# Modulation columns made later: eight column units moved into attention, four into the second feed-forward, and the third group's products reordered

## The chip, the cores and the metric

The kernel runs on one core of one Trainium2 chip. The metric is device time in microseconds (us) of one execution. TensorE is PE in the rows, VectorE DVE, ScalarE ACT, GpSimd POOL; SyncE is SP, which here issues the weight transfers.

## What is computed

A transformer of 256 tokens and width 1024 in fp32. Two layers of a first block come first, each with four mixers side by side (a latent attention, a stick-breaking attention, a block-sparse attention and a gated convolution) and an output product. Then comes a second block: a gated linear attention (GLA), feed-forward 0, an attention of 16 heads in chunks, feed-forward 1. The four stages of the second block are modulated: a vector `c` goes through SiLU and a matrix `w_ada_2`, and gives each stage `s` (0 GLA, 1 feed-forward 0, 2 attention, 3 feed-forward 1) a shift, a scale and a gate. In the reference, cut to that:

```python
...
h = ln(x) * (1 + scale) + shift
x = ln(ALPHA * x + gate * stage(h))
...
```

The shift and scale of a stage are wanted at its input, the gate at its end.

## The kernel before, in words

**The stream of weights.** All weights come as 180 units of 128 x 2048 floats (1 MB) in one fixed order, into a ring `raw` of six slots (`SLOTS = 6`). Unit n goes to slot n % 6. SP issues the units strictly in their order, in one loop at L483: unit n is issued once whoever reads unit n-6 has counted up `used[n % 6]`. So a unit that is read late holds up the issue of the unit six places on, and of all behind that. The strings `ORDER`, `GLA_ORDER`, `FF_ORDER` (and the new `ATT_ORDER`) say what stands where: `w`, `m`, `u` and `d` are weights for TensorE, `a` is a column unit.

**The column units.** `w_ada_2` is 48 of the units. `column_unit` (L982) multiplies a unit with the row `crow` = SiLU(c) on VectorE and sums along the row, in two instructions of 128 x 1024; the second one counts the slot free. No other engine reads these units. Per stage there are eight units for shift and scale (`acc`) and four for the gate (`gacc`); `coefficients(s)` makes the vectors of stage s from its eight, a short operation `gcol` those of its gate from its four. Before, 24 are made in the two layers of the first block (12 each), 11 in GLA, 13 in feed-forward 0, none later.

**Each engine runs its own program** in the written order and waits on semaphores. So where `ada_unit` stands in VectorE's program, everything behind it on VectorE waits for the unit to land and for its two instructions.

**Layer boundary.** At the end of layer 0, `y_norm` gives the new rows, TensorE transposes a tile of 128 tokens (`first_transposes`), ScalarE scales the eight transposed blocks into `hT` (`layer_input`), and TensorE multiplies (`first_units`), tile by tile; `unit_t` of unit `U_CA` comes behind both tiles. `y_square` is a ScalarE operation of the normalisation of the layer that ends.

**GLA's end.** VectorE's program has three column units (8, 9, 10 of GLA), then `mixer_output`, which reads the output product from PSUM; its row results `xs` are what TensorE transposes for feed-forward 0 (L2057).

**Feed-forward.** 16 groups; the products run as seven products of four quarter blocks. Per group TensorE runs of the next group's up products a "first tile", a "half" and a "rest", and of this group's down products part 0 (two products, from the hidden half sums alone) and part 1 (five: one that needs the hidden sums, four that need `weight_sums`, made by VectorE). The "half" waits for the sums of the up weights that VectorE makes in `up_sums` (L1590 to L1595).

**Attention.** Four passes `qd` of four heads. A pass (`four_heads`) runs the scores, softmax, turns (transposes of the probabilities, L1998) and values of four heads, and between them three units `quad_unit(u)` (L2625) that make queries, keys and values of the next pass. GpSimd's program in a pass is `quad_weights(3 qd + 3)` (four sums over the weights of a unit, L578 to L583, once that unit has landed), `head_biases(qd + 1)` (L593 to L596, which ends in a count of `cur_ready`), then `quad_weights` of the next two units. VectorE's program in a pass is: `scores_max`, `head_inverse` of heads 0 and 1, `quad_sums`, `scores_max`, `queries`, `head_inverse` (L1056) of heads 2 and 3, `quad_sums` (L1864 to L1873), `x_piece` or the output weights, `quad_sums`, the copy L1943, `value_rows(qd + 1)` (L1894), which waits for `cur_ready`; then the scores of the next pass (L1046).

Of the kernel before, what the change touches and what calls it, by code (L numbers as in the profile page):

```python
# [14 lines left out]
P = 128  # L15
# [22 lines left out]
A1 = 12  # L38
# [5 lines left out]
ORDER = "wwwawwawwawawawa" "wawawawa" "wwawwa"  # L44
# [37 lines left out]
GLA_ORDER = 4 * "mma" + "mmaaaa" + "mmmmmmaaa"  # L82
FF_ORDER = ("u" + 13 * "uda" + "ud" + "dud", "u" + 14 * "ud" + "dud")
# [3 lines left out]
N_FF1 = N_ATT + 16  # L87
# [10 lines left out]
AG = len(GA_AT)  # L98

ADA_1 = [N_GLA + n for n in GA_AT] + places(FF_ORDER[0], "a", N_FF0)  # L100
assert len(GW_AT) == 16 and len(ADA_1) == 24
# [34 lines left out]
def build(nc, x, units, cols, small, post_g, consts, onehot, rel_bias, crow_in, colb_in,  # L136
          ln_rows, low_in, gk_in, att_line, v_row, out):
    with ExitStack() as ctx:  # L138
# [13 lines left out]
        HB = ((G[2], G[3]), (G[0], G[1]))  # L152
# [114 lines left out]
        early = sb("early", [P, 4, P])  # L267
# [167 lines left out]
        OUT_UNITS.append(tuple(N_ATT + 12 + w for w in range(4)))  # L435
# [7 lines left out]
        OUT_W.append([[ada[:], xs[:, 1, :], row(tline), crow[:]],  # L443
# [46 lines left out]
        def _(pool):  # L490
# [57 lines left out]
            store_gate(0)  # L548
            for l in range(1, DEPTH):
                layer_vectors(l)  # L550
            store_gate(1)

            pool.wait_ge(x_new.sem, 2 * DEPTH + 2)
            for g in range(2):
                load_gate(g)
# [7 lines left out]

            norm_rows(1)
# [4 lines left out]
            def quad_weights(u):  # L569

                n = N_ATT + 3 + u
# [4 lines left out]
                if u >= 3:  # L576
                    wait_used(pool, 0, n - 3)
# [27 lines left out]

            store_gate(3)
            load_gate(3)
# [17 lines left out]
            norm_rows(2)  # L625
            norm_rows(3)

        @block.scalar
        def _(act):
# [79 lines left out]
            for l in range(DEPTH):  # L709
# [201 lines left out]
            def keys(qd):  # L911
                act.wait_ge(bc_ready.sem, bc_ready.at(qd, 1))
                if qd == 0:
                    wait_used(act, 0, N_ATT + 1)
# [42 lines left out]
        def _(dve):  # L957
# [31 lines left out]
            def gate_columns(g, n):  # L989

                wait_used(dve, 0, n)
                dve.wait_ge(colb_ready, 16)
                dve.scalar_tensor_tensor(gcol[:, g, :], gacc[:, g, :], 1.0, colb[:, B_GATE + KC * g:B_GATE + KC * (g + 1)],
                                         ALU.add, ALU.add).then_inc(gcol_ready, 1)

            def ada_unit(l, a):

                n = l * U1 + A_AT[a]
                if a < 4:
                    column_unit(n, gacc[:, l, 2 * a:2 * a + 2])  # L1000
                    if a == 3:
                        gate_columns(l, n)
                else:
                    column_unit(n, acc[:, 0, 16 * l + 2 * (a - 4):16 * l + 2 * (a - 4) + 2])
# [54 lines left out]
            def coefficients(s):  # L1059
# [3 lines left out]
                wait_used(dve, 0, (A_AT[A1 - 1], U1 + A_AT[A1 - 1], ADA_1[19], ADA_1[19])[s])  # L1063
# [104 lines left out]
            for l in range(DEPTH):  # L1168
# [12 lines left out]
                if l > 0:  # L1181
                    ada_unit(l - 1, 11)
                    ada_unit(l, 0)
# [16 lines left out]
                if l == 0:  # L1200
                    silu_row()
                    ada_unit(l, 0)
                ada_unit(l, 1)
# [6 lines left out]
                ada_unit(l, 2)  # L1210
                dve.wait_ge(xg_ready.sem, xg_ready.at(l, 1))
                taps(0, 12)
                ada_unit(l, 3)
# [12 lines left out]
                ada_unit(l, 4)  # L1226
# [12 lines left out]
                ada_unit(l, 5)  # L1239
                ada_unit(l, 6)  # L1240
# [37 lines left out]
                for j in range(2 * H):  # L1278
                    if j % 2 == 0:
# [15 lines left out]
                        if j < 6:  # L1295
                            ada_unit(l, 7 + j // 2)
# [36 lines left out]
                ada_unit(l, 10)  # L1333
# [20 lines left out]
                else:  # L1354
                    ada_unit(l, 11)

            def ada_unit_1(n, idx):

                part, i = idx // 4, idx % 4
                if part in (2, 5):  # L1360
                    g = DEPTH + part // 3
                    column_unit(n, gacc[:, g, 2 * i:2 * i + 2])
                    if i == 3:
                        gate_columns(g, n)
                else:
                    m = (0, 1, 3, 4).index(part)
                    column_unit(n, acc[:, 1, m * KC + 2 * i:m * KC + 2 * i + 2])
# [310 lines left out]

            def groups(s):
# [6 lines left out]
                for g in range(SEVEN - 1):  # L1686
# [8 lines left out]
                    weight_sums(down[g])  # L1695
# [57 lines left out]
            ada_unit_1(ADA_1[0], 0)  # L1753
# [3 lines left out]
            coefficients(1)  # L1757
            ada_unit_1(ADA_1[1], 1)
# [3 lines left out]
            ada_unit_1(ADA_1[2], 2)  # L1762
# [22 lines left out]
            ada_unit_1(ADA_1[3], 3)  # L1785
# [4 lines left out]
            ada_unit_1(ADA_1[4], 4)  # L1790
            mixer_sums(6)
            ada_unit_1(ADA_1[5], 5)
# [22 lines left out]
            for a in (6, 7):  # L1815
                ada_unit_1(ADA_1[a], a)
# [29 lines left out]
            for a in (8, 9, 10):  # L1846
                ada_unit_1(ADA_1[a], a)
# [12 lines left out]
            def quad_sums(u, c):  # L1860

                b = [x[:].rearrange("p (i n) -> p i n", i=4) for x in QUAD_BANKS[u % 3]]
                wait_used(dve, 0, N_ATT + 3 + u)
# [13 lines left out]
            def queries(qd):  # L1877
                dve.wait_ge(bc_ready.sem, bc_ready.at(qd, 1))
                if qd == 0:
                    wait_used(dve, 0, N_ATT)  # L1880
# [1017 lines left out]
```

## Time and profile before

| | |
|---|---|
| median of three runs | 976.6 us (975.53 to 977.18) |
| the profiled execution | 975.87 us, span of its records 974.0 us |
| TensorE busy | 957.1 us, 98% of the span |
| VectorE busy | 758.5 us, 78% |
| ScalarE, GpSimd busy | 230.7 us, 83.7 us |
| moved by DMA | 205.38 MB |

The span runs from the first to the last recorded instruction of the profiled execution; the 1.9 us by which that execution is longer lie around it. Busy time of an engine is the time in which one of its instructions runs. "Idle" in brackets behind a row of a timeline is how long the engine stood still ahead of it, and the name behind the arrow what released it.

### The profile page before, as it was taken

The numbers are of one execution on the slowest core, as the hardware profiler recorded it, in microseconds if no ns is written. First come the engines' busy times: TensorE is split into PE (matmuls) and PEld (weight loads), VectorE is DVE, ScalarE is ACT, GpSimd is POOL, SyncE is SP. The second block draws the span as 40 slices with busy tenths as digits, with TensorE's granted clock in tenths as the row PEclk, the third lists the DMA queues.
The fourth block names the chain that finished last, engine by engine and source line by source line (L and its number), as shares of the span: only waits on it lengthen the run. The fifth ranks groups of instructions, "written<-read, shape, count | busy, mean of one in ns | idle before, by whom it ended". The sixth has DMA issues, their size and how long they took to land. (4 is left out here: it accounts for less than half of the span.)

```text
span 974.0 us, 14339 instructions
## 1 busy us (share of the span) xinstructions
PE 957.1 (98%) x5354; PEld 711.0 (73%) x5354; DVE 758.5 (78%) x1719; ACT 230.7 (24%) x580; POOL 83.7 (9%) x100
## 2 busy tenths in 40 slices
PE   9999999999999999999999999999999999999996
PEld 5858855858857998757777777689994767777764
DVE  2796687696688898999999888955667877766687
ACT  4134425125433222111000000123333200000002
POOL 2100000000001000000001000056830000000000
PEclk9999999999999999999999999999999999999999
DMA  9954653855555766574779777535444254544411
GB/s 354 379 201 191 234 201 149 350 197 226 196 215 209 288 220 257 178 297 149 245 289 336 284 257 259 189 131 195 152 173 147 103 184 173 216 173 174 173 44 44
DMA packets 31069, 205.38 MB, mean 211 GB/s; under 512 B 3640, under 2 KB 4845, under 8 KB 7709
## 3 DMA queue, kind: packets, MB, share of 16 engines
q1 hardware_dynamic: 27740, 190.94, 52.9%
q0 software_dynamic: 3264, 13.57, 3.9%
q8 instruction: 43, 0.70, 0.3%
q14 instruction: 22, 0.17, 0.1%
HBM read 203.42 MB, written 1.07 MB: 210 GB/s over the span
## 5 line engine op out<-in xcount | busy, mean ns | idle before, releaser
L1971 PE MATMUL bank<-hT,raw 128*128 128x256 f32 x736 | 162.5, 380 | 0.0
L1971 PEld LDWEIGHTS bank<-hT,raw 128*128 128x128 f32 x736 | 138.9, 190 | 21.2 <-issue 2.4
L982 DVE CUSTOM_DVE_ANT_0 raw<-raw,crow 128x1024 f32<-128x1024 f32 x96 | 113.2, 1222 | 6.7 <-DMA raw<-units_dram 5.3
L2315 PE MATMUL bank<-yT,arena 128*128 128x512 f32 x224 | 100.8, 593 | 0.1
L2315 PE MATMUL bank<-raw,arena 128*128 128x512 f32 x180 | 86.8, 593 | 0.0
L2315 PEld LDWEIGHTS bank<-yT,arena 128*128 128x128 f32 x224 | 42.5, 190 | 54.0 <-issue 51.9
L2342 PEld LDWEIGHTS bank<-hT,raw 128*128 128x128 f32 x416 | 50.4, 192 | 11.5 <-issue 11.5
L839 ACT ACTIVATE arena<-bank 128x512 f32<-128x512 f32 x26 | 15.6, 598 | 179.3 <-PE bank L2342 179.3
L2342 PE MATMUL bank<-hT,raw 128*128 128x128 f32 x416 | 50.6, 275 | 0.0
L1024 DVE SCALAR_TENSOR_TENSOR arena<-arena 128x256 f32<-128x256 f32 x120 | 49.2, 485 | 0.1
L2342 PE MATMUL bank<-arena 128*128 128x128 f32 x336 | 42.2, 275 | 3.0 <-issue 3.0
L2342 PEld LDWEIGHTS bank<-arena 128*128 128x128 f32 x336 | 39.8, 192 | 4.6 <-issue 4.6
L2342 PE MATMUL bank<-arena,gateT 128*128 128x128 f32 x336 | 42.1, 275 | 0.0
L2315 PEld LDWEIGHTS bank<-raw,arena 128*128 128x128 f32 x180 | 29.9, 191 | 16.3 <-issue 16.3
L2342 PEld LDWEIGHTS bank<-arena,gateT 128*128 128x128 f32 x336 | 39.8, 192 | 0.0
L2040 PE MATMUL bank<-arena 128*128 128x512 f32 x88 | 39.7, 592 | 0.0
L2342 PEld LDWEIGHTS bank<-arena,raw 128*128 128x128 f32 x224 | 29.4, 192 | 13.4 <-issue 13.4
L841 ACT ACTIVATE arena<-bank 128x384 f32<-128x384 f32 x28 | 13.8, 492 | 106.8 <-PE bank L2342 106.8
L2286 PE MATMUL bank<-hT,raw 128*128 128x128 f32 x244 | 37.4, 283 | 1.3 <-ACT hT L700 1.1
L2286 PEld LDWEIGHTS bank<-hT,raw 128*128 128x128 f32 x244 | 33.0, 191 | 4.3 <-issue 3.0
L1602 DVE TENSOR_TENSOR arena<-arena 128x256 f32<-128x256 f32 x26 | 11.4, 440 | 31.0 <-ACT arena L839 30.8
L2040 PEld LDWEIGHTS bank<-arena 128*128 128x128 f32 x88 | 16.6, 190 | 19.8 <-issue 19.7
(471 smaller groups left out, 1767.9 us busy)
## 6 DMA issues: line engine op xcount, KB each, us to landing
raw<-units_dram SPq DMA_DIRECT2D x178, 1024.0 KB, 4.9
arena<-ln_rows_dram POOLq DMA_DIRECT2D x4, 1024.0 KB, 5.0
arena<-gate_scratch POOLq DMA_DIRECT2D x4, 512.0 KB, 5.5
arena<-att_line_dram POOLq DMA_DIRECT2D x4, 512.0 KB, 5.8
arena<-small_dram POOLq DMA_DIRECT2D x2, 896.0 KB, 10.5
raw<-units_dram SPq DMA_DIRECT2D x2, 704.0 KB, 7.5
xt<-x_dram SPq DMA_DIRECT2D x2, 512.0 KB, 5.4
arena<-post_g_dram POOLq DMA_DIRECT2D x2, 512.0 KB, 8.4
```

The source lines that it names most:

```text
L839: act.activation(prod[:, 0:4].rearrange("p i n -> p (i n)"), A[0][:], ACT.Copy).then_inc(prod_ready.sem, 1)
L841: act.activation(prod[:, 4:7].rearrange("p i n -> p (i n)"), A[0][:, 0:3 * P], ACT.Copy).then_inc(prod_ready.sem, 1)
L982: ins = dve.tensor_tensor_reduce(out=w, in0=w, in1=crow[:], scale=1.0, scalar=0.0, op0=ALU.mult, op1=ALU.add, accum_out=dst[:, c:c + 1])
L1024: ins = dve.scalar_tensor_tensor(cacc[:, c, :], xg[:, c, j:j + S], w, cacc[:, c, :], ALU.mult, ALU.add)
L1602: ch.do(dve.tensor_tensor(csum[:, 0:5:4], p[:, 0:1].to_broadcast([P, 2, P]), p[:, 1:3], ALU.add))
L1971: mm = pe.matmul(b[:, c * S:(c + 1) * S], raw[:, s, k * 256 + c * P:k * 256 + (c + 1) * P], act_t[:, k, :], start=(k == 0), stop=(k == KC ...
L2040: mm = pe.matmul(OUT_BANKS[l][j][:], x[c] if isinstance(x, list) else x[:, c], y[c] if isinstance(y, list) else y[:, 512 * c:512 * (c + 1) ...
L2286: mm = pe.matmul(b[:, c * S + t * P:c * S + (t + 1) * P], raw[:, n % SLOTS, k * 256 + c * P:k * 256 + (c + 1) * P], hT[:, k, t * P:(t + 1) ...
L2315: mm = pe.matmul(SB[i][:], x, y, start=g == 0, stop=stop)
L2342: mm = pe.matmul(b[:, i * P:(i + 1) * P], x(k), y(k), start=k == 0, stop=k == 3)
```

## The change

Column units are numbered through all four stages now (`ADA_AT`, `ada_unit(i)`): the two layers of the first block make six each (GLA's twelve), GLA makes twelve (feed-forward 0's), feed-forward 0 twelve (attention's), attention eight (shift and scale of feed-forward 1), feed-forward 1 four (its own gate). In attention they stand behind `head_inverse` of head 3: two in pass 0, three in pass 1, three in pass 2. `coefficients` 1, 2 and 3 move with them. At the layer boundary `layer_input` is issued in two halves around the second `y_square`, and `U_CA`'s product is made per tile (`first_columns`), its first half ahead of the second tile's transposes. At GLA's start the second tile's transposes are issued two products earlier. In the feed-forwards' group 1 the two products of part 0 are issued ahead of the "half", and the product with the hidden sums ahead of the "rest"; VectorE makes `weight_sums` of that group a group earlier. Two small loads of the gate rows (`store_gate`, `load_gate`) move later on GpSimd.

```diff
-A1 = 12
+A2 = 12
+A1 = 6
...
-ORDER = "wwwawwawwawawawa" "wawawawa" "wwawwa"
+ORDER = "wwwawwa" "wwwawwa" "wwawwa" "wwww"
...
-GLA_ORDER = 4 * "mma" + "mmaaaa" + "mmmmmmaaa"
-FF_ORDER = ("u" + 13 * "uda" + "ud" + "dud", "u" + 14 * "ud" + "dud")
+GLA_ORDER = 4 * "mma" + "mmaaaa" + "mmmmmmaaaa"
+ATT_ORDER = "www" "aa" "wwwa" "aa" "wwwa" "aa" "wwwwwww"
+FF_ORDER = ("u" + 2 * "ud" + "aua" + 10 * "dua" + "du" + "ddud",
+            "u" + 2 * "ud" + "aua" + 2 * "dua" + 9 * "du" + "ddud")
...
+ATT_UNITS = ((0, 1), (2, 3, 4), (5, 6, 7), ())
...
-        HB = ((G[2], G[3]), (G[0], G[1]))
+        HB = ((G[2], G[3]), (A[2], A[3]))
...
                     y_square(l, 1, 0)
+                    layer_input(l + 1, 0, 0, KC // 2)
                     y_square(l, 1, 1)
-                    layer_input(l + 1, 0, 0, KC)
+                    layer_input(l + 1, 0, KC // 2, KC)
...
+            def ada_unit(i):
+
+                n, g, j = ADA_AT[i], i // A2, i % A2
+                if j < 2 * H:
+                    column_unit(n, acc[:, g // 2, 16 * (g % 2) + 2 * j:16 * (g % 2) + 2 * j + 2])
                 else:
-                    column_unit(n, acc[:, 0, 16 * l + 2 * (a - 4):16 * l + 2 * (a - 4) + 2])
+                    column_unit(n, gacc[:, g, 2 * (j - 2 * H):2 * (j - 2 * H) + 2])
+                if j == A2 - 1:
+                    wait_used(dve, 0, n)
+                    dve.wait_ge(colb_ready, 16)
+                    dve.scalar_tensor_tensor(gcol[:, g, :], gacc[:, g, :], 1.0, colb[:, B_GATE + KC * g:B_GATE + KC * (g + 1)],
+                                             ALU.add, ALU.add).then_inc(gcol_ready, 1)
...
+            def side_unit(lay, g):
+
+                if g < (AH - AF0, len(ADA_AT) - AF1)[lay]:
+                    ada_unit((AF0, AF1)[lay] + g)
+                    if lay == 0 and g == 2 * H - 1:
+                        coefficients(2)
...
                     up_half_sums(s, g + 1)
-                    weight_sums(down[g])
+                    if g == 1:
+                        side_unit(lay, 0)
+                    else:
+                        weight_sums(down[g])
                     up_rest_sums(s, g + 1)
                     hidden_sums(s, g + 1, (g + 1) % 3)
                     if g < SEVEN - 2:
                         up_sums(up[g + 2], g + 2)
                     else:
                         weight_sums(down[SEVEN - 1], wsum_last)
+                    if g == 0:
+                        wait_used(dve, 0, down[0])
+                        weight_sums(down[1])
                     if 1 <= g <= 4:
                         x_piece(s - 1, g - 1)
...
-                    if lay == 0 and AG + g < len(ADA_1):
-                        ada_unit_1(ADA_1[AG + g], AG + g)
-                        if AG + g == len(ADA_1) - 1:
-                            coefficients(2)
-                            coefficients(3)
+                    if g > 0:
+                        side_unit(lay, g)
...
-            coefficients(1)
-            ada_unit_1(ADA_1[1], 1)
...
             for a in (6, 7):
-                ada_unit_1(ADA_1[a], a)
+                ada_unit(GA + a)
+            coefficients(1)
...
-            for a in (8, 9, 10):
-                ada_unit_1(ADA_1[a], a)
+            for a in (8, 9, 10, 11):
+                ada_unit(GA + a)
 
             mixer_output(MIXER, MIX_S, OUT_BANKS[MIXER])
...
                 head_inverse(h0, 3)
+                for a in ATT_UNITS[qd]:
+                    ada_unit(AH + a)
+                    if a == 2 * H - 1:
+                        coefficients(3)
                 if qd == H - 2:
                     dve.wait_ge(oq_ready.sem, 2)
                     out_inputs(HEADS, 0)
...
+            def first_columns(turns, n, b, t):
+
+                wait_landed(pe, turns, n)
+                for c in range(2):
+                    for k in range(KC):
+                        mm = pe.matmul(b[:, c * S + t * P:c * S + (t + 1) * P],
+                                       raw[:, n % SLOTS, k * 256 + c * P:k * 256 + (c + 1) * P],
+                                       hT[:, k, t * P:(t + 1) * P], start=(k == 0), stop=(k == KC - 1))
+                if t == NT - 1:
+                    mm.then_inc(used[n % SLOTS], 1)
...
                     first_units(l, t)
+                    if l > 0 and t == 0:
+                        first_columns(T1 * l, U_CA, G[0], t)
...
-                unit_t(T1 * l, U_CA, hT, G[0])
+                if l > 0:
+                    first_columns(T1 * l, U_CA, G[0], 1)
+                else:
+                    unit_t(T1 * l, U_CA, hT, G[0])
...
-                if part != 0:
+                if part != 0 and stage != "weights":
                     pe.wait_ge(hsum_ready.sem, hsum_ready.at(s // 2, g + 1))
                     product(2, hsum[:, k, 3], b[1][1])
+                if part != 0 and stage != "input":
...
                     if g > 1:
                         up_products(s, n, g + 1, "first tile")
+                    if g == 1:
+                        seven_products(s, down[g], g, 0)
                     if g > 0:
                         up_products(s, n, g + 1, "half")
-                    seven_products(s, down[g], g, 0)
+                    if g == 1:
+                        seven_products(s, down[g], g, 1, stage="input")
+                    else:
+                        seven_products(s, down[g], g, 0)
                     up_products(s, n, g + 1, "rest")
-                    seven_products(s, down[g], g, 1)
+                    seven_products(s, down[g], g, 1, stage="weights" if g == 1 else None)
...
                 for k in range(KC):
+                    if t == 0 and k == KC - 2:
+                        input_transposes(1)
                     mm = unit_columns(n, G[1], t, 1)(k)
                 if t == NT - 1:
                     mm.then_inc(used[n % SLOTS], 1)
-                if t == 0:
-                    input_transposes(1)
```

The engines' programs show where instructions went. First VectorE in pass 0 of attention, before: `head_inverse` of heads 2 and 3 (L1056), then at once `quad_sums` (L1864 on).

```order
L1056 RECIPROCAL rinv<-rsum 128x2 x2
L1864 COPY arena<-bank 128x128
L1866 TENSOR_TENSOR arena<-arena,bank 128x2x128
L1868 TENSOR_TENSOR arena<-arena,bank 128x128
L1869 TENSOR_TENSOR arena<-arena,bank 128x128
```

The same place of VectorE's program after the change; L991 is `column_unit`, with two rows for each of its instructions (the second reads out the sum), L1530 is `x_piece`.

```order
L1061 RECIPROCAL rinv<-rsum 128x2 x2
L991 ISA raw,acc<-raw,crow 128x1024
L991 ISA acc 128x1
L991 ISA raw,acc<-raw,crow 128x1024
L991 ISA acc 128x1
L991 ISA raw,acc<-raw,crow 128x1024
L991 ISA acc 128x1
L991 ISA raw,acc<-raw,crow 128x1024
L991 ISA acc 128x1
L1860 COPY arena<-bank 128x128
L1862 TENSOR_TENSOR arena<-arena,bank 128x2x128
```

Two whole column units now stand between the two. In passes 1 and 2 there are three at that place.

Next TensorE at the boundary from layer 0 to layer 1, before: L2012 are the transposes of a tile, L2024 its first units, L1971 are `unit_t` of U_CA, U_CG and U_BQ.

```order
L2012 MATMUL bank<-kst,xs 128x128 x8
L2024 MATMUL bank<-raw,hT 128x352 x8
L2012 MATMUL bank<-kst,xs 128x128 x8
L2024 MATMUL bank<-raw,hT 128x352 x8
L1971 MATMUL bank<-hT,raw 128x256 x48
```

After, with `first_columns` as L2036:

```order
L2012 MATMUL bank<-kst,xs 128x128 x8
L2024 MATMUL bank<-raw,hT 128x352 x8
L2036 MATMUL bank<-hT,raw 128x128 x16
L2012 MATMUL bank<-kst,xs 128x128 x8
L2024 MATMUL bank<-raw,hT 128x352 x8
L2036 MATMUL bank<-hT,raw 128x128 x16
L1971 MATMUL bank<-hT,raw 128x256 x32
```

Sixteen of the 48 products have moved, in two halves by tile, one of them between the tiles.

## Rows read from the trace of the kernel before

**Rows 1.** The page's first part: busy us, share of the span, instructions.

```profile
PE 957.1 (98%) x5354; PEld 711.0 (73%) x5354; DVE 758.5 (78%) x1719; ACT 230.7 (24%) x580; POOL 83.7 (9%) x100
```

**Rows 2.** TensorE's waits: us in total, times, longest.

```profile
PE bank L2024 <- ACT hT L685: 1.5, 2, 1.3
PE bank L2286 <- ACT hT L700: 1.1, 3, 0.4
PE bank L2057 <- DVE xs L1419: 0.2, 1, 0.2
```

**Rows 3.** VectorE: first unit at GLA's end, what follows; first operation of `coefficients(3)`.

```profile
413.97 1.22 DVE L982 CUSTOM_DVE_ANT_0 raw<-raw,crow 128x1024 f32<-128x1024 f32 x1
420.84 0.69 DVE L1153 COPY arena<-bank 128x512 f32<-128x512 f32 x1
607.88 0.18 DVE L1065 TENSOR_TENSOR arena<-acc,colb 128x16 f32<-128x16 f32 x1 [0.21 <-DVE arena L1079]
```

**Rows 4.** Attention, pass 0 into pass 1: start, us, engine, line.

```profile
667.40 1.28 POOL L578 TENSOR_TENSOR arena<-raw 128x512 f32<-128x512 f32 x1 [5.49 <-PE bank L2625]
672.43 0.47 POOL L593 COPY arena<-arena 128x256 f32<-128x256 f32 x1
673.94 0.30 POOL L596 MEMSET arena<- 64x256 f32 x1
676.12 0.29 DVE L1864 COPY arena<-bank 128x128 f32<-128x128 f32 x1 [3.34 <-PE bank L2625]
678.62 2.26 POOL L581 TENSOR_TENSOR gateT<-gateT,raw 128x512 f32<-128x512 f32 x1
685.50 1.83 DVE L1894 TENSOR_TENSOR arena<-arena 128x256 f32<-128x256 f32 x2
686.39 1.95 PE L2625 MATMUL bank<-arena 128*128 128x128 f32 x16
690.86 0.91 PE L1998 MATMUL bank<-kst,probs 128*128 128x128 f32 x6
```

**Rows 5.** The weight queue: one issue; landing times, single and of two issued together.

```profile
417.62 0.33 SPq L483 DMA_DIRECT2D raw<-units_dram  x1
DMA to landing us min/median/max: 4.6/4.6/4.6
DMA to landing us min/median/max: 4.8/5.8/6.8
```

**Rows 6.** Pass 1 into pass 2; window: length, PE, PEld, DVE, ACT, POOL busy.

```profile
696.54:709.36 12.82, 12.82 (x117) 12.05 (x116) 7.60 (x16) 3.25 (x8) 11.39 (x10) 1.00 0.47 150
709.36 1.83 DVE L1894 TENSOR_TENSOR arena<-arena 128x256 f32<-128x256 f32 x2
```

**Rows 7.** Pass 2 into pass 3, from the end of `head_inverse` to the scores.

```profile
719.78:733.89 14.11, 14.11 (x118) 12.54 (x117) 9.82 (x23) 2.96 (x8) 0.85 (x3) 1.00 0.54 194
733.89 0.28 DVE L1046 CUSTOM_DVE_ANT_0 probs<-bank,arena 128x128 f32<-128x128 f32 x1
```

**Rows 8.** TensorE at the layer boundary.

```profile
158.09 1.13 PE L2024 MATMUL bank<-raw,hT 128*128 128x352 f32 x3 [1.32 <-ACT hT L685]
```

**Rows 9.** Feed-forward 0, group 1: TensorE, VectorE and ScalarE around the half.

```profile
456.81 0.69 DVE L1595 TENSOR_TENSOR arena<-raw,arena 128x512 f32<-128x512 f32 x1
457.61 2.02 PE L2342 MATMUL bank<-arena 128*128 128x128 f32 x16 [1.51 <-issue]
464.72 3.60 PE L2315 MATMUL bank<-yT,arena 128*128 128x512 f32 x8
464.06 0.49 ACT L841 ACTIVATE arena<-bank 128x384 f32<-128x384 f32 x1 [4.01 <-PE bank L2342]
469.03 0.69 DVE L1595 TENSOR_TENSOR gateT<-raw,gateT 128x512 f32<-128x512 f32 x1
```

**Rows 10.** Windows at the end of the span; the number before DMA's is the granted clock.

```profile
966.00:970.00 4.00, 0.00 (x0) 0.00 (x0) 3.73 (x12) 1.54 (x3) 0.00 (x0) 0.98 0.32 131
970.00:974.00 4.00, 0.00 (x0) 0.00 (x0) 1.46 (x3) 0.00 (x0) 0.00 (x0) 0.50 0.35 131
```

More of the change, by code:

```diff
@@ L97 @@
 GW_AT, GA_AT = places(GLA_ORDER, "m"), places(GLA_ORDER, "a")
-AG = len(GA_AT)
-ADA_1 = [N_GLA + n for n in GA_AT] + places(FF_ORDER[0], "a", N_FF0)
-assert len(GW_AT) == 16 and len(ADA_1) == 24
+ATT_UNITS = ((0, 1), (2, 3, 4), (5, 6, 7), ())
+ATT_AT = places(ATT_ORDER, "w", N_ATT)
+ADA_AT = [l * U1 + n for l in range(DEPTH) for n in A_AT] + [N_GLA + n for n in GA_AT]
+GA, AF0 = DEPTH * A1, len(ADA_AT)
+ADA_AT += places(FF_ORDER[0], "a", N_FF0)
+AH = len(ADA_AT)
+ADA_AT += places(ATT_ORDER, "a", N_ATT)
+AF1 = len(ADA_AT)
+ADA_AT += places(FF_ORDER[1], "a", N_FF1)
+assert len(GW_AT) == len(ATT_AT) == 16 and (AF0, AH, AF1, len(ADA_AT)) == (24, 36, 44, 48)
 RE = 2 * DEPTH
@@ L434, in build @@
         OUT_UNITS = DEPTH * [(U_O0, U_O1, U_O2, U_O3)] + [tuple(N_GLA + GW_AT[12 + w] for w in range(4))]
-        OUT_UNITS.append(tuple(N_ATT + 12 + w for w in range(4)))
+        OUT_UNITS.append(tuple(ATT_AT[12 + w] for w in range(4)))
         MIXER, HEADS = DEPTH, DEPTH + 1
@@ L547, in _ @@
             pool.tensor_copy(moba_bias[:], zline[:, :, ::-1]).then_inc(fixed_ready, 1)
-            store_gate(0)
             for l in range(1, DEPTH):
                 layer_vectors(l)
-            store_gate(1)
+            store_gate(0)
             pool.wait_ge(x_new.sem, 2 * DEPTH + 2)
-            for g in range(2):
-                load_gate(g)
+            load_gate(0)
             pool.dma_start(ln_row[:].rearrange("p g d -> p (g d)"), ln_rows[0, :, :].to_broadcast([P, 2 * D])).then_inc(lnrow_in, 16)
@@ L625, in _ @@
             norm_rows(2)
+            store_gate(3)
+            load_gate(3)
             norm_rows(3)
@@ L1353, in _ @@
                     x_scale(l + 1, 1)
[L1354 to L1367, printed above, removed]
             def stage_tiles(s, b=None):
@@ L2306, in unit_columns, with seven_products @@
                 return column
-            def seven_products(s, n, g, part=None, stop=False, wsum=wsum):
+            def seven_products(s, n, g, part=None, stop=False, wsum=wsum, stage=None):
                 k = g % 3
@@ L2723, in last_heads @@
                 out_product(HEADS, 1, 3)
[L2725 to L2726 removed]
+            wait_landed(pe, 0, ATT_AT[2])
+            unit_tile(2, ATT_AT[0], A[3], 0, value_column(0), held=2)
             stage_tile(2, 1)
[L2728 to L2730 removed]
+            unit_rest(ATT_AT[0], A[3], 0, 2)
+            unit_tile(2, ATT_AT[0], A[3], 1)
+            unit_t(0, ATT_AT[1], hT, G[1])
             for k in range(KC):
                 mm = value_column(1)(k)
[L2733 removed]
+            mm.then_inc(used[ATT_AT[2] % SLOTS], 1)
             for qd in range(H - 1):
@@ L2815, in lay_out @@
     cols, small = [], []
+    ada = []
+    for g in range(2 * DEPTH):
+        w, p = i["w_ada_2"][g // 2], 3 * (g % 2)
+        ada += [ada_columns(w, p + a // 4, a % 4) if a < 8 else ada_gate(w, p + 2, a - 8) for a in range(A2)]
     for l in range(DEPTH):
@@ L2827, in lay_out @@
         for a, n in enumerate(A_AT):
-            w = i["w_ada_2"][0]
-            layer[n] = ada_gate(w, 3 * l + 2, a) if a < 4 else ada_columns(w, 3 * l + (a - 4) // 4, a % 4)
+            layer[n] = ada[A1 * l + a]
         units += layer
@@ L2840, in lay_out @@
             i["conv_pw_w"][l].reshape(2, P, GW).transpose(1, 0, 2).reshape(P, 512)], 1))
-    ada1 = [ada_gate(i["w_ada_2"][1], a // 4, a % 4) if a // 4 in (2, 5) else ada_columns(i["w_ada_2"][1], a // 4, a % 4)
-            for a in range(6 * D // 256)]
     w, wo = i["gla_w_in_2"][0], i["gla_w_out_2"][0]
@@ L2848, in lay_out @@
     part = [None] * len(GLA_ORDER)
-    for n, u in zip(GW_AT + GA_AT, ws + ada1[:AG]):
+    for n, u in zip(GW_AT + GA_AT, ws + ada[GA:AF0]):
         part[n] = u
@@ L2855, in lay_out @@
         f2 = [w2[256 * g:256 * (g + 1)].reshape(2, P, D).transpose(1, 0, 2).reshape(P, UNIT) for g in range(GROUPS)]
-        rest = {"u": iter(f1), "d": iter(f2), "a": iter(ada1[AG:])}
+        rest = {"u": iter(f1), "d": iter(f2), "a": iter(ada[(AF0, AF1)[l]:])}
         units += [next(rest[c]) for c in FF_ORDER[l]]
@@ L2859, in lay_out @@
             w, wo = i["att_w_in_2"][0], i["att_w_out_2"][0]
-            for qd in range(H):
-                units += [t_unit(w, part * D + GW * qd) for part in range(3)]
-            units += [n_unit(wo, 512 * c, half) for half in range(2) for c in range(2)]
+            ws = [t_unit(w, part * D + GW * qd) for qd in range(H) for part in range(3)]
+            ws += [n_unit(wo, 512 * c, half) for half in range(2) for c in range(2)]
+            rest = {"w": iter(ws), "a": iter(ada[AH:])}
+            units += [next(rest[c]) for c in ATT_ORDER]
     b_ada, b_in = i["b_ada_2"].reshape(DEPTH, 6, D), i["att_b_in_2"][0].reshape(3, D)
```

75 lines of the change are left out of this document (27 added, 48 removed).

## The prediction

> **What bounds the kernel now.** I read the page's first part first: TensorE is busy for 98% of the span, VectorE for 78% [rows 1]. Then TensorE's waits, which are few and short [rows 2]; the chain of waits gives nearly all to TensorE too. So the time can only fall by those few waits, some 4 us, and it grows as soon as anything else makes TensorE wait. Whether the change does that has to be read from the places where column units now stand. There I asked three things of the timeline: when VectorE is free, when the next unit of weights is issued and lands, and when TensorE first needs what comes of it.
>
> **Price of a column unit.** At GLA's end three units fill the time from 413.97 to 420.84 [rows 3]: 6.87 us, 2.29 each. The work is the same 48 units before and after, so what counts is where they stand and when they free their slot of the ring.
>
> **Attention, pass 0.** VectorE finishes head 3's inverse at 672.78 (676.12 less 3.34 idle) and then waits for TensorE [rows 4]. Two units take it to 672.78 + 4.58 = 677.36, 1.24 past the time at which it went on before. That alone is mostly absorbed. The ring is the trouble: in the new order the units read `aa www a` at this place, so column units 3 and 4 stand directly ahead of the fourth weight unit (u = 3), and unit 4 can be issued only when column unit 1's slot is free, at 677.36. With about 0.15 for the semaphore and 0.5 for an issue (an estimate: one issue took 0.33 [rows 5]) weight unit 3 is issued at 678.0. It is the second of two transfers in flight; the second of such a pair landed after 6.8 us, a lone one after 4.6 [rows 5]. So it lands at 684.8. Before, it had long landed: GpSimd began its four sums on it at 667.40, ended them at 672.43 (5.03 us), and ended `head_biases` at 674.24, 1.81 later [rows 4]. Now the sums run from 684.8 to 689.8 and the biases to 691.6. Two instructions pay for that. TensorE's product with these sums stood at 686.39, so it waits 3.4 there; and `value_rows` on VectorE, at 685.50 before, waits for the biases to 691.6, 6.1 late [rows 4]. Queued behind `value_rows` are the next pass's scores, and behind those the turns at 690.86 [rows 4]. Between the two chains there is no idle time of TensorE that could soak it up. The sum of pass 0 is **+6.1** (the 3.4 lies inside it).
>
> **Pass 1.** The window from head 3's inverse to `value_rows`, 696.54 to 709.36, starts at 702.6 now. Three units end at 702.6 + 6.87 = 709.5. The seventh weight unit (u = 6) stands right behind column unit 7, which waits for the slot of the third of these three: it is issued at 710.2, lands at 717.0 by the same 6.8, its sums are done at 722.0 and the biases at 723.8. `value_rows` stood at 709.36 [rows 6]: it is 14.4 late, so pass 1 adds **+8.3**. Here VectorE's own excess would have been 6.87 less the window's idle 12.82 − 7.60 = 5.22, that is 1.65 [rows 6]; the ring, not VectorE, ends last.
>
> **Pass 2.** No weight sums follow it on GpSimd, so only VectorE counts. Its window has 14.11 − 9.82 = 4.29 us idle [rows 7]. Added are 6.87 and `coefficients(3)`, four short operations of about 0.18 with a wait of 0.21 before them [rows 3], 0.9 together; nothing hides them at this place. If all idle time is used the delay is 6.87 + 0.9 − 4.29 = 3.5, and I take **+3.8**, since the last piece of idle time can't be used wholly before TensorE's next unit. The scores at 733.89 move by 18.2 in all.
>
> **GLA's end.** A fourth unit there costs 2.29, the gate's short operation `gcol` 0.2 (of the same kind), and `coefficients(1)`, now in this busy stretch, 0.7 without that wait: 3.2 if the unit has landed. It hasn't: its slot is that of an output weight unit, which the queue refilled at 417.62; 4.6 later is 422.2 [rows 5]. The unit ends at 424.5, `gcol` at 424.9, and the copy that stood at 420.84 starts 4.1 late [rows 3]. TensorE's transposes for feed-forward 0 already waited for the end of that chain (the line L2057 of [rows 2]), so nothing covers it. **+4.1**, with 3.2 as lower bound.
>
> **What is removed.** At the layer boundary TensorE stood still for 1.32 us ahead of 158.09 [rows 8], since ScalarE ran `y_square` first; the second layer's input now goes ahead of it for the first half, and the first columns cover the other tile. **−1.3**. At GLA's start the waits sum to 1.1 in three pieces, the longest 0.4 [rows 2]; the earlier transposes cover one: **−0.4**, with 0 and −1.1 as bounds. In group 1 of each feed-forward TensorE stood 1.51 us ahead of the half [rows 9], because the up sums end at 456.81 + 0.69 = 457.50. Two products of 0.86 each (two matmuls of 512 columns; eight took 3.60 [rows 9], 0.43 start to start) now stand in that gap, so it goes. But they are then missing after the rest, where they used to cover the next sums: those are ready 469.03 + 0.69 − 464.06 = 5.7 after ScalarE starts [rows 9], and TensorE now has four products, 3.4, and a first tile, 1.7, for it. A new wait of 0.6 takes the place of part of the old one. Net −1.0, twice: **−2.0**. The bounds are −3.0 and 0. Moving eight units out of the first two layers and others between GLA and feed-forward 0 is put at nothing: TensorE shows no wait there that a column unit ends, and it costs nothing while VectorE stays ahead of it. The four units in feed-forward 1 are hidden likewise, in groups that had the same units in feed-forward 0.
>
> **The sum.** 6.1 + 8.3 + 3.8 + 4.1 − 1.3 − 0.4 − 2.0 = +18.6. The profiled execution took 975.87 (974.0 span and 1.9 around it): 994.5. It lies 0.7 below the median 976.6, so against that 995.2. I predict **995**. Bounds of the pieces: if both weight units land after 4.6 instead of 6.8, −4.4; if GLA's unit is there in time, −0.9; the gains' bounds are −1.7 and +2.4. Above: one of GpSimd's sums took 2.26 instead of 1.28 while VectorE read two inputs beside it [rows 4], two such in each pass make +4 at most. The likeliest case by itself spans 989 to 1000.
>
> **Rivals.**
> *A, the clock.* Several of the new waits last about 4 us. At the end of the span TensorE's granted clock is 0.98 in the first 4 us without a matmul and 0.50, the lower of its two levels, in the next [rows 10]. If a wait in attention or at GLA's end lets it fall, each microsecond at the lower level does half a microsecond's work; 4 us of it behind a wait, as much as the last window shows, cost 2 us each, 2 to 6 in all: 997 to 1001. Against it: the waits come in pieces of 3 to 4 us with matmuls between. The Trainium skill's page "TensorE: Matmul & The Clock Gate", Part 1, says that throttled is the default and that activity releases it; the trace agrees that the clock falls after work ends, and by that page the matmuls behind a long wait would run at half rate. Chance 0.15.
> *B, the ring holds nothing up.* If weight units 3 and 6 land in time after all (a slot free earlier than I read), only VectorE's excess remains: 1.65 + 3.5 + 4.1 − 3.7 = +5.6: 982. Against it stands the order `aa www a`, by which SP cannot pass a column unit that waits. Chance 0.09.
> *C, faster.* The column units in attention run wholly in VectorE's idle time, and the fourth unit at GLA's end too. VectorE is idle for 22% of the span [rows 1], and if the pieces fit, only the gains are left: 975.9 − 3.7 + 0.7 = 973. It decides at pass 0: the gap there is 3.34, two units need 4.58 [rows 4], so it needs 1.2 us of slack behind it, and more in passes 1 and 2. Chance 0.05.
> *D, the change gives nothing,* all parts hidden or cancelled, within 0.2%: 0.02.
>
> **The numbers.** My own case 0.69. With A it makes 0.84 between 985 and 1003, the range I give; it leaves out B, C and D. A measurement of this kernel tells 0.2%, about 2 us, from no change. Faster by more than that 0.05, within it 0.03, slower 0.92.
>
> **What would show it.** In the profile after, the attention stage: VectorE's unit instructions behind head 3's inverse in passes 0 to 2; the weight unit behind each group issued right after the group's last unit, GpSimd's sums starting only at its landing, some 17 us later than before in pass 0; TensorE's waits at L2625's successor for GpSimd's sums and at the turns, 3 to 8 us in all in each of two passes. At GLA's end TensorE waits some 4 us for `xs`. At the layer boundary and ahead of the first half in both feed-forwards no wait over 0.3, and a new one of some 0.6 ahead of the next half. The prediction is wrong if the weight units of attention are issued well before the column units ahead of them are read, or if GpSimd's sums are not what `value_rows` waits for.

## The result, and the profile after

The changed kernel took 1008.91 us (median of 4, 1007.93 to 1009.6) where the kernel before took 976.74 beside it: a ratio of 1.0332, 95% interval 1.0317 to 1.0346. It is slower by 32.2 us; 995 was predicted, with 1003 as the upper end. The direction and most of the places were right, the sum of 18.6 was 13.6 too small.

The page's first part and TensorE's waits after the change (us in total, times, longest), which answer to [rows 1] and [rows 2]:

```profile
PE 968.7 (96%) x5386; PEld 721.0 (72%) x5386; DVE 762.3 (76%) x1719; ACT 230.6 (23%) x580; POOL 79.8 (8%) x100
...
PE bank L1998 <- ACT probs L652: 11.2, 3, 6.2
PE bank L2647 <- POOL arena L592: 4.6, 2, 3.2
PE bank L2068 <- DVE xs L1405: 4.1, 2, 3.9
PE bank L2647 <- DMA raw<-units_dram: 2.8, 1, 2.8
PE bank L2647 <- DVEq L1871: 2.4, 1, 2.4
```

TensorE's work is the same, in 32 more instructions because sixteen products are halved. It waits some 21 us more in attention (L1998, L2647) and 4 us at GLA's end (L2068). It is also busy 11.6 us longer: its mean granted clock is 0.982 of full speed, before it was 0.998. The span splits at the first products of a stage. Feed-forward 0 and all ahead of it end 2.9 us later than before (attention's first product stands at 640.12, before at 637.23). Attention takes 157.0 us to the first product of feed-forward 1 at 797.15, before 125.2: +31.8. Feed-forward 1 gives 0.9 back. Those make the 33.8 between the two spans. The profiled execution is the slowest of the four, 1009.6 us; in two later profiles of the same kernel attention takes 154.6 and 155.1, so that a term of about 2 us in this profile can be chance.

Attention from pass 0 into pass 1, in rows of the timeline that answer to [rows 4]; SP's row is the issue of weight unit 3, and its landing time stands below it:

```profile
680.40 0.33 SPq L492 DMA_DIRECT2D raw<-units_dram  x1
DMA to landing us min/median/max: 7.0/7.0/7.0
687.48 1.27 POOL L587 TENSOR_TENSOR arena<-raw 128x512 f32<-128x512 f32 x1 [18.00 <-DMA raw<-units_dram]
692.68 2.02 PE L2647 MATMUL bank<-arena 128*128 128x128 f32 x16 [3.17 <-POOL arena L592]
693.92 0.31 POOL L605 MEMSET arena<- 64x256 f32 x1
694.26 6.14 DVE L1890 TENSOR_TENSOR arena<-arena 128x256 f32<-128x256 f32 x2 [5.78 <-POOL arena L605]
703.59 1.59 PE L1998 MATMUL bank<-kst,probs 128*128 128x128 f32 x6 [6.21 <-ACT probs L652]
```

Read from the top: the unit is issued only when the column units ahead of it have been, and lands 7.0 later at 687.4; GpSimd had stood still for 18 us and starts its sums at once; TensorE waits 3.17 for them; `head_biases` ends at 694.2, and `value_rows`, which had waited 5.78 for it, begins. All this is as forecast: 694.26 is 8.8 later than before, of which 2.3 are the later start of the pass (head 3's inverse ends at 675.04, before at 672.78), so +6.5 against +6.1. But then the two instructions of `value_rows` take 6.14 us, where they took 1.83 [rows 4]; beside them GpSimd runs the sums of the next unit. The turn comes 12.7 later than before instead of 8.8. TensorE's waits for sums, landing and turn add up to 9.4 in pass 0 and 8.5 in pass 1, above the 3 to 8 of the forecast.

Passes 1 and 2, which answer to [rows 6] and [rows 7]:

```profile
DMA to landing us min/median/max: 8.7/8.7/8.7
726.15 1.27 POOL L587 TENSOR_TENSOR arena<-raw 128x512 f32<-128x512 f32 x1 [20.69 <-DMA raw<-units_dram]
732.94 6.13 DVE L1890 TENSOR_TENSOR arena<-arena 128x256 f32<-128x256 f32 x2 [8.63 <-POOL arena L605]
...
761.74 1.22 DVE L1134 TENSOR_TENSOR ada<-raw 128x1024 f32<-128x1024 f32 x1 [2.30 <-DMA raw<-units_dram]
768.61 0.28 DVE L1051 CUSTOM_DVE_ANT_0 probs<-bank,arena 128x128 f32<-128x128 f32 x1
```

The same happens once more: unit 6 lands 8.7 us after its issue, and the rows take 6.13. In pass 2 VectorE waits 2.30 for an output weight unit, queued behind the last column units; in the two later profiles this wait is 0.91 and 0.95. GLA's end, the boundary and the clock, which answer to [rows 3], [rows 8] and [rows 10]; in the windows the granted clock is the number ahead of DMA's share:

```profile
420.69 1.23 DVE L991 CUSTOM_DVE_ANT_0 raw<-raw,crow 128x1024 f32<-128x1024 f32 x1 [0.83 <-DMA raw<-units_dram]
423.19 0.69 DVE L1158 COPY arena<-bank 128x512 f32<-128x512 f32 x1
433.33 1.97 PE L2068 MATMUL bank<-kst,xs 128*128 128x128 f32 x8 [3.89 <-DVE xs L1405]
428.00:432.00 4.00, 1.44 (x4) 0.37 (x2) 3.47 (x9) 0.29 (x1) 0.00 (x0) 0.98 0.96 390
432.00:436.00 4.00, 2.67 (x10) 2.15 (x11) 3.83 (x7) 1.45 (x5) 0.00 (x0) 0.50 1.00 394
436.00:440.00 4.00, 4.00 (x23) 3.48 (x22) 3.50 (x6) 1.45 (x5) 0.00 (x0) 0.67 1.02 430
...
156.62 2.60 PE L2024 MATMUL bank<-raw,hT 128*128 128x352 f32 x8
```

The fourth unit waits for its landing (0.83) and TensorE for `xs` (3.89), as forecast; behind that wait the clock is 0.50, and the eight transposes take 1.97, where eight such took 1.04 to 1.09 with the clock at 1.00, its upper level. The boundary's wait is gone: the first units follow the transposes, and no idle time stands behind the row at 156.62. In group 1 of feed-forward 0 the new wait stands where it was forecast, ahead of the next half, and has the forecast size:

```profile
473.14 2.02 PE L2359 MATMUL bank<-arena,gateT 128*128 128x128 f32 x16 [0.58 <-issue]
```

### The profile page after: what moved, and what is told of

It is laid out like the page before. It is cut to its first block and busy times, and to the rows that moved or that the text cites. A ratio compares the mean times of both kernels' runs of the same rounds, so it can differ in the third digit from the quotient of the medians.

```text
span 1007.8 us, 14402 instructions
## 1 busy us (share of the span) xinstructions
PE 968.7 (96%) x5386; PEld 721.0 (72%) x5386; DVE 762.3 (76%) x1719; ACT 230.6 (23%) x580; POOL 79.8 (8%) x100
## 5 line engine op out<-in xcount | busy, mean ns | idle before, releaser
L1971 PE MATMUL bank<-hT,raw 128*128 128x256 f32 x704 | 155.6, 380 | 0.0
L1971 PEld LDWEIGHTS bank<-hT,raw 128*128 128x128 f32 x704 | 132.7, 190 | 20.1 <-issue 2.4
L991 DVE CUSTOM_DVE_ANT_0 raw<-raw,crow 128x1024 f32<-128x1024 f32 x96 | 113.9, 1231 | 12.5 <-DMA raw<-units_dram 11.2
L2359 PEld LDWEIGHTS bank<-hT,raw 128*128 128x128 f32 x416 | 50.4, 192 | 11.5 <-issue 11.5
L2359 PEld LDWEIGHTS bank<-arena 128*128 128x128 f32 x336 | 39.8, 192 | 1.2 <-issue 1.2
L2302 PEld LDWEIGHTS bank<-hT,raw 128*128 128x128 f32 x244 | 33.3, 194 | 4.0 <-issue 2.9
L536 POOL DMA_DIRECT2D gate_scratch<-gcol x4 | 2.2, 554 | 382.6 <-DVE gcol L1008 382.6
```

Source lines behind the costliest of these rows:

```text
L991: ins = dve.tensor_tensor_reduce(out=w, in0=w, in1=crow[:], scale=1.0, scalar=0.0, op0=ALU.mult, op1=ALU.add, accum_out=dst[:, c:c + 1])
L1971: mm = pe.matmul(b[:, c * S:(c + 1) * S], raw[:, s, k * 256 + c * P:k * 256 + (c + 1) * P], act_t[:, k, :], start=(k == 0), stop=(k == KC ...
L2302: mm = pe.matmul(b[:, c * S + t * P:c * S + (t + 1) * P], raw[:, n % SLOTS, k * 256 + c * P:k * 256 + (c + 1) * P], hT[:, k, t * P:(t + 1) ...
L2359: mm = pe.matmul(b[:, i * P:(i + 1) * P], x(k), y(k), start=k == 0, stop=k == 3)
```

## The experiments

**The ring.** The first run: the order of attention's units alone:

```diff
-ATT_ORDER = "www" "aa" "wwwa" "aa" "wwwa" "aa" "wwwwwww"
+ATT_ORDER = "wwwwww" "aa" "www" "aaa" "www" "aaa" "wwww"
```

> The changed kernel with one string altered: the weight units of attention come ahead of the column units (six weights, two columns, three weights, three columns, three weights, three columns, four weights). VectorE's program is the same. Theory (the ring delays the weights): weight units 3 and 6 land in time, GpSimd's sums are early, VectorE's long rows operation goes back to under 2 us, no wait of TensorE for GpSimd; attention costs only VectorE's own excess, 1.65 + 3.8, so 982 to 986 us. Rival (VectorE has no room for eight units in attention): stays above 1000 us.

991.91 us, ratio 1.0158 (1.0141 to 1.0175) to the kernel before beside it. 17 us go with one string, so the ring is the largest part; but 6 us more are left than expected. TensorE's waits, VectorE's and GpSimd's rows in pass 1 and TensorE's next product:

```profile
PE bank L2647 <- DVEq L1871: 8.4, 3, 4.5
...
702.41 2.28 DVE L991 CUSTOM_DVE_ANT_0 raw<-raw,crow 128x1024 f32<-128x1024 f32 x1
701.36 2.25 POOL L588 TENSOR_TENSOR arena<-raw 128x512 f32<-128x512 f32 x1
714.24 1.46 PE L2647 MATMUL bank<-raw,arena 128*128 128x128 f32 x8 [4.49 <-DVEq L1871]
```

GpSimd is no longer waited for. Instead TensorE waits for VectorE, which drains a unit (`quad_sums`) only behind its three column units, and these run beside GpSimd's early sums: 2.28 us instead of 1.22, and a sum takes 2.25 instead of 1.27.

**GpSimd's sums beside VectorE.** The same kernel with the sums replaced by a fill:

```diff
-                ch.do(pool.tensor_tensor(d[:, 0], a[1][0], a[1][1], ALU.add))
-                ch.do(pool.tensor_tensor(d[:, 2], a[0][0], a[1][0], ALU.subtract))
-                ch.sync(1)
-                ch.do(pool.tensor_tensor(d[:, 1], d[:, 0], a[0][0], ALU.subtract))
-                ch.sync()
-                pool.tensor_tensor(d[:, 3], a[0][1], d[:, 1], ALU.subtract).then_inc(asum_ready, 1)
+                pool.memset(d, 0.0).then_inc(asum_ready, 1)
```

> The first run (weights ahead of the columns in the ring) with GpSimd's four sums of each unit replaced by one fill with zeros: the sums are left out, waits and counts stay. In the first run TensorE never waited for GpSimd, so an earlier end of GpSimd's work cannot help by itself. Theory (VectorE's column units and row operations ran at half pace beside GpSimd's sums): the column instructions take 1.22 us everywhere instead of up to 2.28, TensorE's wait of 4.5 in pass 1 shrinks to about 0.5, that of 0.9 in pass 0 goes, the 3.1 in pass 2 stays: 982 to 986 us. Rival (VectorE's longer instructions come from the transfers into the ring, not from GpSimd): 990 to 993 as in the first run.

985.59 us, ratio 1.0100 (1.0084 to 1.0116), 6.3 below the first run. VectorE's value rows of pass 0, a column instruction of pass 1, and TensorE's product that had waited 4.49:

```profile
689.11 0.75 DVE L1885 TENSOR_TENSOR arena<-arena 128x256 f32<-128x256 f32 x2
700.67 1.22 DVE L986 CUSTOM_DVE_ANT_0 raw<-raw,crow 128x1024 f32<-128x1024 f32 x1
709.33 1.16 PE L2642 MATMUL bank<-raw,arena 128*128 128x128 f32 x8 [1.71 <-DVEq L1866]
```

The rows take 0.75, the columns 1.22 (one, beside GpSimd's copy of the biases, 2.04), and the wait is 1.71. What is left is 9 us over the kernel before: attention starts 3.6 later, behind GLA's end, and itself takes 6.6 longer, while feed-forward 1 gives 0.9 back. The 6.6 stand where VectorE's own excess was forecast at 1.65 and 3.8, and TensorE waits 4.8 of them for VectorE's draining. Neither term hangs on the order of attention's units.

**The rows alone.** In the changed kernel, GpSimd waits for the value rows ahead of the next unit's sums:

```diff
                 if qd < H - 2:
+                    pool.wait_ge(v4_ready.sem, v4_ready.at(qd + 1, 2))
                     quad_weights(3 * qd + 4)
```

> The changed kernel with one wait added: GpSimd starts the sums of each pass's second unit only when VectorE has made the value rows. Theory (the two engines get in each other's way, so that value rows took 6.1 us instead of 0.75): the rows take 0.75 to 0.8 in passes 0 and 1, TensorE's waits ahead of the turns shrink by 5.3 each, and some of the low clock behind them goes: 993 to 998 us. Rival (all of the delay is the late landing, the long rows operation only fills time in which TensorE would wait anyway): 1007 to 1010.

1001.03 us, ratio 1.0259 (1.0242 to 1.0276): 7.9 below the changed kernel's 1008.9. VectorE's row and TensorE's waits:

```profile
694.34 0.76 DVE L1891 TENSOR_TENSOR arena<-arena 128x256 f32<-128x256 f32 x2 [5.83 <-POOL arena L605]
...
PE bank L2648 <- DVEq L1872: 8.5, 2, 5.4
```

The rows take 0.76 in both passes, but the time is 3 us above the expected range: with the turns earlier, TensorE now waits 8.5 for the draining behind the column units. That wait stood at 2.4 in the changed kernel, where TensorE was late itself. The 1001.0 lie inside the predicted range, whose upper end is 1003.

**GpSimd's order.** The biases ahead of the sums of the pass's first unit:

```diff
-                if qd < H - 2:
-                    quad_weights(3 * qd + 3)
                 pool.wait_ge(nm_ready.sem, HE + H * qd + H)
                 head_biases(qd + 1)
                 if qd < H - 2:
+                    quad_weights(3 * qd + 3)
                     quad_weights(3 * qd + 4)
```

> The changed kernel with GpSimd's program reordered in each pass: the head biases ahead of the sums of the first unit. The late landing stays. Theory (the chain landing, sums, biases, value rows, scores sets the time): only TensorE's own waits for the landing and for the sums are left, some 3.3 in pass 0 and 7 to 8 in pass 1; value rows take under 1 us in time; 994 to 1000 us. Rival (TensorE's direct wait for the sums is the one that counts, the rows lie inside it): 1006 to 1010.

1000.46 us, ratio 1.0251 (1.0234 to 1.0269): 0.5 above the expected upper end, far from the rival. TensorE's direct waits for sums and landing are still there, 8.3 in all, and no wait ahead of a turn is left among TensorE's longest: the rest of the late landing's cost went through the biases, the rows and the turns.

**GLA's fourth unit.** The new order, and the unit made in feed-forward 0:

```diff
-GLA_ORDER = 4 * "mma" + "mmaaaa" + "mmmmmmaaaa"
+GLA_ORDER = 4 * "mma" + "mmaaaa" + "mmmmmmaaa"
...
-FF_ORDER = ("u" + 2 * "ud" + "aua" + 10 * "dua" + "du" + "ddud",
+FF_ORDER = ("u" + 2 * "ud" + "aua" + 11 * "dua" + "ddud",
...
-            for a in (8, 9, 10, 11):
+            for a in (8, 9, 10):
```

> As the first, and the fourth column unit at GLA's end goes back into feed-forward 0 (eleven in GLA, thirteen there). Theory: TensorE's 4 us at GLA's end go, and with them the low clock behind, some 1.5 to 2 us: 5.5 to 6 us below the first run, 977 to 980 us. Rival (the wait there only moves into the first groups of feed-forward 0): within 2 us of the first run.

989.21 us, ratio 1.0133 (1.0103 to 1.0164), 2.7 below the first run, where 5.5 to 6 were expected and the rival said less than 2. Its runs spread from 986 to 992.5. In the profiles TensorE's 4 us at GLA's end are gone and attention starts 3.9 earlier, but attention itself is 0.9 longer. The intervals of the two runs overlap, so neither the size nor the choice between the two expectations is settled; that the wait goes, and attention starts earlier, is seen in one profile of each.

**What the change's other parts bring.** The kernel before, with only the reordered products of group 1; only the boundary and GLA's start; both. The edits are those of the diff above, at the same lines.

> The kernel before with the reordered products of group 1 in both feed-forwards alone (column units and VectorE's program as before). Theory: the 1.5 us wait ahead of the half goes in each, a wait of about 0.6 comes ahead of the next half: net 1.0 each, 974.5 to 975.2 us. Rival (the wait comes back whole at the next half, since the work behind it only changes place): 976.5.

> The kernel before with the layer boundary's edits (layer input ahead of the second square, first columns by tile) and the earlier transposes at GLA's start alone. Theory: 1.0 to 1.3 and 0.4 to 0.5 less: 974.8 to 975.4 us. Rival (the second tile's chain becomes the bound at the boundary): 976.5.

> The kernel before with both of these sets of edits and no column unit moved. Theory: the gains add, 3.2 to 3.7 less than before: 973.0 to 973.6 us. Rival (one of them is given back later, for instance in the ring): 975 or more.

974.74 us, ratio 0.9984 (0.9975 to 0.9993); 974.91, ratio 0.9984 (0.9975 to 0.9993); 973.00, ratio 0.9969 (0.9957 to 0.9981), against 976.21 beside them. The gains are clear of the noise, and within it they add: 1.5, 1.3 and 3.2 us. TensorE in group 1 of feed-forward 0, with both:

```profile
454.80 1.88 PE L2332 MATMUL bank<-raw,arena 128*128 128x512 f32 x4
456.51 1.98 PE L2360 MATMUL bank<-arena 128*128 128x128 f32 x16
462.41 3.70 PE L2332 MATMUL bank<-yT,arena 128*128 128x512 f32 x8 [0.38 <-DVE yT L1640]
467.84 2.02 PE L2360 MATMUL bank<-arena,gateT 128*128 128x128 f32 x16
```

The two products at 454.80 fill the old gap, and the half follows at 456.51 without one. The new wait is 0.38, ahead of the four products and not of the next half (467.84 has none): they wait for `weight_sums` (L1640), which VectorE makes behind the column unit here. These runs leave out the part of the change that makes `weight_sums` of this group a group earlier; with it, in the changed kernel, the wait is the 0.58 ahead of the next half. With 973.0 us this kernel is faster than both the kernel before and the changed one.

**The clock.** Idle TensorE filled with matmuls of no use, first at GLA's end, then in attention:

```diff
+                if s == 1 and t == 0:
+                    for i in range(32):
+                        pe.transpose(G[3][:, 0:P], ident, ident)
                 pe.wait_ge(xn_ready.sem, xn_ready.at(s - 1, t + 1))
```

```diff
+                if u == 6:
+                    for i in range(20):
+                        pe.transpose(b[0][:, 0:P], ident, ident)
                 wait_landed(pe, 0, n)
...
+                if u in (3, 6):
+                    for i in range(26):
+                        pe.transpose(b[0][:, 2 * P:3 * P], ident, ident)
                 pe.wait_ge(quad_tsum, 1)
...
+                if h0 in (HE + H, HE + 2 * H) and j == 0:
+                    pe.wait_ge(pt_ready.sem, h0 + j - 1)
+                    for i in range(36):
+                        pe.transpose(b[:, 0:P], ident, ident)
                 pe.wait_ge(pn_ready.sem, h0 + j + 1)
```

> The changed kernel with 32 matmuls of 128 columns into a free PSUM bank ahead of TensorE's wait at GLA's end; they take about 3.4 of the 4 us in which TensorE waits there anyway, their result is not used. Theory (the low clock behind that wait costs time of its own): the granted clock stays at the upper level there, the matmuls behind take their usual time, 1.5 to 2.2 us less than the changed kernel. Rival (the work at the low clock is hidden behind VectorE's output rows): no difference above 0.5 us.

> The changed kernel once more, on the chip of the run before it, as its reference: 1008 to 1010 us.

> The changed kernel with matmuls of no use ahead of TensorE's waits in attention: 26 ahead of its wait for GpSimd's sums in passes 1 and 2 (units 3 and 6), 20 ahead of the wait for the landing of unit 6, 36 ahead of the first turn of passes 1 and 2; each set is shorter than the wait that it stands in, the results are not used. Theory (behind these waits the matmuls run at the lower level of the clock, and that is a term of its own beside the waits): the low stretches in passes 0 and 1 go, 4 to 5 us less than the changed kernel run beside it, so 1003 to 1005. Rival (the slow matmuls lie beside a chain through GpSimd and VectorE that ends later anyway): within 1 us of the changed kernel.

> The changed kernel again, as the reference on the same chip: 1007 to 1010 us.

The first gave 1007.87 us against 1007.96 of the changed kernel beside it, the second 1008.60 against 1008.13. The first time is what its rival expected, but its profile doesn't settle why: the clock at GLA's end is 1.00 throughout and attention starts 1.2 us earlier than beside it, though the fourth unit's work ended 0.8 later in that profile; attention then took 1.7 longer, which is within what attention varies by from profile to profile. The second decides for the rival. Windows of it and of the changed kernel beside it, between GpSimd's first sums and the turn:

```profile
692.00:696.00 4.00, 3.63 (x33) 3.42 (x33) 0.00 (x0) 0.00 (x0) 3.92 (x5) 1.00 0.59 242
696.00:700.00 4.00, 4.00 (x38) 4.00 (x38) 2.77 (x1) 0.00 (x0) 3.92 (x5) 1.00 0.32 108
```

```profile
692.00:696.00 4.00, 2.96 (x14) 2.99 (x15) 1.38 (x1) 0.00 (x0) 3.92 (x6) 0.50 0.05 18
696.00:700.00 4.00, 4.00 (x26) 4.00 (x26) 4.00 (x2) 0.00 (x0) 3.92 (x4) 0.66 0.39 131
```

With the clock at 1.00 instead of 0.50 and 0.66 there, attention took 154.9 us to the first product of feed-forward 1, against 155.1. Behind the added matmuls TensorE still waited 4.9 ahead of the turns, against 9.7 without them, so they didn't hold it up there. TensorE's slow matmuls lie beside GpSimd's sums and VectorE's slow rows, which end later either way. A slow stretch behind each turn was left in both kernels (six transposes took 1.59 in pass 0 of this run too, against 0.91 before); what that costs, no run shows.

## Why the prediction was too low

The rows of values once more in the kernel before, at the end of pass 2:

```profile
733.22 0.75 DVE L1894 TENSOR_TENSOR arena<-arena 128x256 f32<-128x256 f32 x2
```

- **Pass 0**, +6.1: the chain of slot, issue, landing, sums, biases and rows is confirmed by the run with the new order and by the one with the biases first, and its size was 6.5. **The step that failed** is the next one, that the scores and turns are simply queued behind `value_rows` at its old duration. The rows took 6.14 instead of 1.83, since GpSimd's delayed sums now run beside them: +4.3, and the same 4.3 in pass 1. The run in which GpSimd waits for the rows takes it away (0.76), and the one without the sums shows where it comes from. That there was such a price could be read before: [rows 4] hold 1.83 for two instructions that take 0.75 at 733.22, where GpSimd is idle. I read the slow row of GpSimd there as GpSimd's risk alone and put it in the upper bound, not VectorE's. The size was not in reach: the old rows show 1.1 of it, not 5.4.
- **Pass 1**, +8.3: the same step, and the landing was mis-sized. The stretch from head 3's inverse to the rows grew by 10.4, since unit 6 took 8.7 us, not 6.8 (8.5 and 8.8 in the later profiles). Two units issued ahead of it were still in flight. So were two in pass 0, where unit 3 took 7.0: that the 6.8 of a pair came near it was luck.
- **Pass 2**, +3.8: the stretch from the inverse to the scores grew by 6.1. VectorE's excess was right, but it then waited 2.30 for an output weight unit behind the column units, which I had not priced.
- **Attention as a whole**, +18.2: 6.5, 10.4, twice 4.3 and 6.1 are 31.6 of attention's 31.8; the stretches between them make the remaining 0.2. That is 13.6 above the forecast, of which 8.6 are the rows. In the two later profiles the excess is between 11 and 12, with the same slow rows.
- **GLA's end**, +4.1: right, 3.9 (the prediction's own terms, 424.5 and 0.2, give 3.9 too). Attention starts 2.9 late instead of the 1.4 that the terms give (4.1 − 1.3 − 0.4 − 1.0). The clock behind the wait is the likely cause, since attention started 1.2 earlier in the profile where it was kept up; no difference of times shows it.
- **What is removed**, −3.7: 3.2 when alone. In group 1 the net is 0.75 each, not 1.0; the new wait in the changed kernel is 0.58, as forecast.
- **Rivals.** The clock fell as rival A's mechanism has it, but in attention it is nearly all hidden. The Trainium skill's page "TensorE: Matmul & The Clock Gate", Part 1, says that the clock is throttled unless activity releases it; the 0.50 behind the wait at GLA's end agrees. Rival B is what the new order makes, where the ring no longer binds: 991.9, not its 982. The contention of the two engines is 6.3 of that difference (985.6 without the sums). Rival C is excluded: with the ring's delay and the contention both gone, 9 us over the kernel before remain.

## What to carry to other kernels

In a ring of slots issued in order, work that "only fills idle time" also stands in the queue: price the unit behind it, through every engine that waits for that unit, before pricing the work itself. When a delay moves one engine's work in time, look at what then runs beside it; an instruction's old duration holds only for its old neighbours. And a wait taken away may uncover the next one, so the waits of one profile don't add up to a gain.

## What the runs showed of the hardware

VectorE and GpSimd slow each other. Two 128x256 sums on VectorE took 0.75 to 0.76 alone and 6.13 to 6.14 beside GpSimd's 128x512 sums, which stayed at 1.27 to 1.45; column instructions of 128x1024 and GpSimd's sums beside them went from 1.22 and 1.27 both to about 2.25. The Trainium skill's page "GPSIMD Engine Reference", section "Key points", says that GpSimd shares its SBUF interfaces with VectorE and contends with instructions that have two SBUF inputs; the traces agree. What decides whether one engine pays or both was not tested. The 6.14 look like standing still rather than like a slower pace:

```profile
L1890 DVE TENSOR_TENSOR arena<-arena x2: 1482/3108/4733, 694.3 to 698.9; 128x256 f32<-128x256 f32 x2
697.42 1.27 POOL L590 TENSOR_TENSOR gateT<-gateT,raw 128x512 f32<-128x512 f32 x1
698.77 1.34 POOL L592 TENSOR_TENSOR gateT<-raw,gateT 128x512 f32<-128x512 f32 x1
```

The first row (ns, shortest, median and longest) has the two instructions of pass 0: the one that starts at 694.26 took 4.73 and ended at 698.99, 0.3 after the third of three GpSimd sums without a gap between them; the second took 1.48 and ended 0.3 after the fourth. In the kernel before, the two instructions ended at 687.33, also 0.3 behind the end of a sum, but of only one, which began with them at 685.52. No run was made to tell standing still from a slower pace.

Weight units issued close together landed one after another. In pass 1 five issues at 712.3, 714.6, 716.8, 717.4 and 718.6 landed after 5.0, 6.6, 6.7, 8.7 and 9.9 us, where a lone one took 4.6 [rows 5]; the last four landed 2.3 to 2.6 us apart.
